# Hybrid decoder block with a mixture of experts: the final norm of all rows started before the last item's result, the last item's rows normed apart and scattered into the output

## What is computed

```python
x = x + mixed @ w_out[l]
x = x + moe(rms_norm(x, norm_ffn_g[l]), router_w[l], ...)   # top 4 of 32 experts
return rms_norm(x, final_norm_g)
...
gu = xb @ w_gu[e] + b_gu[e]
glu = jnp.minimum(gu[:, :D_FF], SWIGLU_LIMIT)
lin = jnp.clip(gu[:, D_FF:], -SWIGLU_LIMIT, SWIGLU_LIMIT)
act = glu * jax.nn.sigmoid(SWIGLU_ALPHA * glu) * (lin + 1)
return act @ w_down[e] + b_down[e]
```

## Time and profile before

| | us |
|---|---|
| median of 3 runs | 2394.51 (2391.37 to 2397.74) |
| the profiled execution, its own time | 2396.7 |
| its span | 2395.0 |
| TensorE matmul busy | 2314.8 (97%) |
| VectorE busy | 762.6 (32%) |
| ScalarE busy | 612.7 (26%) |
| GpSimd busy | 252.7 (11%) |
| clock that TensorE was granted, mean share | 0.987 |

### The profile page before, as it was taken

One profiled execution on the slowest core, in us unless ns is written; L12 is line 12 of the kernel. 1 busy time (PEld: TensorE's weight loads), 2 busy tenths in 40 slices (PEclk: granted clock), 3 DMA queues, 4 the chain that ended last, 5 costly groups with the idle time before them and its releaser, 6 DMA issues.

```text
span 2395.0 us, 41347 instructions
## 1 busy us (share of the span) xinstructions
PE 2314.8 (97%) x15446; PEld 1990.1 (83%) x15447; DVE 762.6 (32%) x1822; ACT 612.7 (26%) x1286; POOL 252.7 (11%) x231
## 2 busy tenths in 40 slices
PE   7999999999999999999999999999999999999993
PEld 4444554556589999999999999989999999999993
DVE  2342222678552233223322233212222222232222
ACT  2123121344312222222222232212222222222223
POOL 1000000111220010011001010000000000011001
PEclk9999999999999999999999999999999999999997
DMA  8000000211178999899898699846877787798785
GB/s 292 35 1 0 0 36 35 95 54 51 51 253 246 287 293 297 267 291 295 279 282 282 216 291 299 290 138 204 283 231 229 228 274 241 238 292 273 220 257 198
DMA packets 440781, 486.44 MB, mean 203 GB/s; under 512 B 24316, under 2 KB 417708, under 8 KB 440700
## 3 DMA queue, kind: packets, MB, share of 16 engines
q1 hardware_dynamic: 420140, 450.33, 57.2%
q0 software_dynamic: 20368, 35.29, 7.1%
q10 hardware_dynamic: 224, 0.16, 0.0%
HBM read 474.49 MB, written 49.58 MB: 219 GB/s over the span
## 4 chain that ended last, share of the span: by engine, by line
PE 95%; issue 2%; DVE 1%; DMA 1%; ACT 1%; POOL 0%; SPq 0%; ACTq 0%; POOLq 0%; DVEq 0%
PE PS L989 66%; PE PS L626 14%; PE PS L822 5%; PE PS L955 2%; PE PS L913 2%; PE PS L795 1%; PE PS L762 1%; PE PS L784 1%; PE PS L707 0%; PE PS L704 0%; PE PS L841 0%; DMA out_dram<-unit 0%; DVE unit L1489 0%; PE PS L662 0%; PE PS L599 0%
## 5 line engine op out<-in xcount | busy, mean ns | idle before, releaser
L989 PE MATMUL PS<-pairA,unit 128*128 x12288 | 1583.6, 291 | 13.8 <-issue 12.3
L989 PEld LDWEIGHTS PS<-pairA,unit 128*128 128x128 f32 x12288 | 1557.1, 191 | 34.3 <-issue 22.6
L626 PE MATMUL PS<-pairA,unit 128*128 128x512 f32 (+1 forms) x528 | 233.4, 598 | 2.8 <-issue 2.8
L1752 DVE TENSOR_SCALAR unit<-PS,cur_b 128x256 f32<-128x256 f32 x256 | 112.1, 480 | 353.3 <-PE PS L989 353.2
L1267 ACT ACTIVATE unit<-PS,cur_b 128x256 f32<-128x256 f32 x256 | 107.5, 471 | 454.9 <-PE PS L989 454.9
L542 POOL DMA_INDIRECT unit<-h_dram,cur_x x66 | 68.5, 1038 | 1301.6 <-DVE cur_x L1748 1212.9
L1254 ACT ACTIVATE unit<-unit 128x512 f32<-128x512 f32 x128 | 80.7, 631 | 466.0 <-DVE unit L1752 466.0
L626 PEld LDWEIGHTS PS<-pairA,unit 128*128 128x128 f32 (+1 forms) x528 | 97.9, 189 | 120.8 <-issue 120.1
L1258 ACT ACTIVATE unit<-PS,cur_b 128x256 f32<-128x256 f32 x256 | 107.5, 471 | 316.1 <-PE PS L989 316.1
L1759 DVE TENSOR_SCALAR unit<-unit 128x512 f32<-128x512 f32 x128 | 54.7, 427 | 339.5 <-ACT unit L1258 339.2
L1741 DVE COPY cur_b<-b_all 128x24 f32 x32 | 5.7, 178 | 437.7 <-ACT unit L1267 433.8
(11 more groups left out here) (242 smaller groups left out, 1257.5 us busy)
## 6 DMA issues: line engine op xcount, KB each, us to landing
unit<-in_expert_w_gu_dram SPq DMA_DIRECT2D x256, 1024.0 KB, 5.3
unit<-in_expert_w_down_dram SPq DMA_DIRECT2D x128, 1024.0 KB, 6.9
unit<-in_w_in_dram SPq DMA_DIRECT2D x6, 2048.0 KB, 15.4
pairB<-in_x_dram SPq DMA_DIRECT2D x16, 512.0 KB, 6.7
unit<-in_w_out_dram SPq DMA_DIRECT2D x2, 2048.0 KB, 9.5
h_dram<-pairA SPq DMA_DIRECT2D x8, 512.0 KB, 2.6
acc_dram<-pairB SPq DMA_DIRECT2D x8, 512.0 KB, 3.5
pairB<-acc_dram SPq DMA_DIRECT2D x8, 512.0 KB, 7.4
```

The source lines that it names most:

```text
L626: ins = pe.matmul(ps, lhs, rhs, start=(k == 0), stop=(k == KD - 1))
L989: ins = pe.matmul(bank(s)[:, ITEM * j:ITEM * j + w], slot_w[s][:, k, P * j:P * j + P], xa_cols[:, ITEM * k:ITEM * k + KD * ITEM + w][:, ba ...
L1752: ins = dve.tensor_scalar(glu_t[:, c % 2, ITEM * j:ITEM * j + ITEM], bank(gate_slot)[:, ITEM * j:ITEM * j + ITEM], cur_b[:, 2 * c + j:2 * ...
```

## The change

- SyncE waits for `y_sent` of last + 1 instead of last + 2 before the tail's loads: for all scatters but the one with the last item's result.
- That last scatter is gone. GpSimd instead gathers the last item's rows from `acc_dram` into SBUF (`last_rows`, cleared by a memset near the start of the items). VectorE adds the last result times the gate there straight from PSUM (`add_last`, four pieces of 512), after the norm of tile 4. ScalarE squares these rows, VectorE and GpSimd make their factors, VectorE scales them into `last_out`, and after all 8 tiles' stores have landed GpSimd scatters them into the output, over the rows that the tiles' stores wrote without the last item's share.
- VectorE itself squares and sums tiles 0 to 4 (`tensor_tensor_reduce`); ScalarE does tiles 5 to 7.
- In `one_pass` the registers and turns now stand in front of the pass's matmuls instead of behind them: no turn before pass 0, `turn_y` before pass 1, `turn_rows` before pass 2. The order of matmuls and turns on TensorE is thereby the same as before.
- The last `turn_y` is written out twice: directly behind the loop where there are no further items, and behind the code for them.

```diff
-            sp.wait_ge(y_sent, last + 2)
+            sp.wait_ge(y_sent, last + 1)
...
-            scatter(last)
+            pool.wait_ge(cur_y_ready, last + 1)
+            pool.sem_inc(pool_waited, 1)
+            for b in range(2):
+                pool.indirect_dma_start(
+                    out=last_rows[:, b, :], out_offset=None, in_=acc_dram,
+                    in_offset=bass.IndirectOffsetOnAxis(ap=cur_y[:, b:b + 1], axis=0),
+                    bounds_check=last_x, oob_is_err=False).then_inc(xg_in, 16)
             for t in range(NT):
                 pool.wait_ge(mean_sq, 3 * NT + t + 1)
...
+            pool.wait_ge(mean_sq, 4 * NT + 1)
+            pool.tensor_tensor(small[:, 4:6], small[:, 0:2], neg_half[:, 0:2], ALU.pow).then_inc(rstd_ready, 1)
+            for i in range(3):
+                pool.wait_ge(out_sent[i], 16 * len(range(i, NT, 3)))
+            for b in range(2):
+                pool.wait_ge(out_ready, NT + b + 1)
+                pool.sem_inc(pool_waited, 1)
+                pool.indirect_dma_start(
+                    out=out_flat, out_offset=bass.IndirectOffsetOnAxis(ap=cur_y[:, b:b + 1], axis=0),
+                    in_=last_out[:, b, :], in_offset=None,
+                    bounds_check=last_x, oob_is_err=False).then_inc(y_out, 16)
...
             def one_pass(widths):
+
+                p = pe.snap(phase, min_val=0, max_val=2)
+                with pe.If(p < 1):
...
+                with pe.Else():
+                    nxt = pe.snap(item, min_val=1, max_val=ITEMS)
+                    with pe.If(p < 2):
...
+                            turn_y()
...
+                    with pe.Else():
...
+                            turn_rows(nxt)
...
                 by_width(n, widths, four_slabs)
...
+            def turn_last():
+                pe.wait_ge(rhs_ready, 8 * last + 4)
+                for s in range(SLOTS):
+                    pe.wait_ge(bank_read[s], 48 * last + 16)
+                turn_y()
...
-            with pe.If(last > N_EXP):
+            with pe.If(last <= N_EXP):
+                turn_last()
+            with pe.Else():
...
+                turn_last()
...
-            take_y(last)
-
-            for t in range(NT):
+            for t in range(DVE_TILES, NT):
                 act.wait_ge(rows_in[t], 32)
...
+            for b in range(2):
+                act.wait_ge(last_summed, 2 * b + 2)
+                act.wait_ge(sum_squared, NT - DVE_TILES + b)
+                act.activation(sum_squares[:, 1, :], last_rows[:, b, :], ACT.Square,
+                               accum_out=small[:, b:b + 1]).then_inc(sum_squared, 1)
...
+            def add_last():
+
+                dve.wait_ge(xg_in, 32 * last + 96)
+                dve.wait_ge(g_ready, last + 1)
+                for q in range(4):
+                    dve.wait_ge(y_ps, 4 * last + q + 1)
+                    rows = last_rows[:, q // 2, HALF * (q % 2):HALF * (q % 2) + HALF]
+                    dve.scalar_tensor_tensor(out=rows, in0=bank(4 + q), scalar=g_now[:, q // 2, :], in1=rows,
+                                             op0=ALU.mult, op1=ALU.add).then_inc(last_summed, 1)
...
                 tail_norm(t)
+                if t == DVE_TILES - 1:
+                    add_last()
```

More of the change, by code:

```diff
@@ L89, in build @@
     out_rows = out.rearrange("b (t p) d -> (b t) p d", p=P)
+    out_flat = out.rearrange("b s d -> (b s) d")
     w_in_k = w_in.rearrange("l (k p) n -> p (l k) n", p=P)
@@ L551, in _ @@
             gather(0)
+            pool.wait_ge(xT_ps, 4)
+            step.do(pool.memset(last_rows, 0.0))
             pool.wait_ge(items_ready, 2)
@@ L970, in _ @@
                 "n_last", "n_now", "n_next", "phase", "moved", "first_six", "all_eight", "half", "pe_item"))
-            pe.load(n_now, item_n[0:1, 0:1])
-            pe.reg_mov(n_last, SEQ)
-            for reg, value in ((moved, 16), (first_six, 4), (all_eight, 4), (half, 0), (phase, 0), (item, 0), (n_next, 0)):
+            pe.load(n_next, item_n[0:1, 0:1])
+            pe.reg_mov(n_now, SEQ)
+            for reg, value in ((moved, 16), (first_six, 4), (all_eight, 0), (half, 0), (phase, 0), (item, 0), (n_last, SEQ)):
                 pe.reg_mov(reg, value)
             def one_pass(widths):
+                p = pe.snap(phase, min_val=0, max_val=2)
+                with pe.If(p < 1):
+                    pe.reg_mov(n_last, n_now)
+                    pe.reg_mov(n_now, n_next)
+                    pe.reg_add(item, item, 1)
+                    pe.reg_add(all_eight, all_eight, 4)
+                    pe.reg_mov(first_six, all_eight)
+                    pe.reg_mov(half, 0)
+                    pe.reg_mov(phase, 1)
+                with pe.Else():
+                    nxt = pe.snap(item, min_val=1, max_val=ITEMS)
+                    with pe.If(p < 2):
+                        n_done = pe.snap(n_last, min_val=0, max_val=SEQ)
+                        with pe.If(n_done <= P):
+                            turn_y(1)
+                        with pe.Else():
+                            turn_y()
+                        pe.load(n_next, item_n[0:1, bass.ds(nxt, 1)])
+                        pe.reg_mov(phase, 2)
+                    with pe.Else():
+                        n_after = pe.snap(n_next, min_val=0, max_val=SEQ)
+                        pe.wait_ge(y_evac, 4 * nxt)
+                        with pe.If(n_after <= P):
+                            turn_rows(nxt, 1)
+                        with pe.Else():
+                            turn_rows(nxt)
+                        pe.reg_add(first_six, all_eight, 3)
+                        pe.reg_add(all_eight, all_eight, 4)
+                        pe.reg_mov(half, KD * ITEM)
+                        pe.reg_mov(phase, 0)
                 n = pe.snap(n_now, min_val=0, max_val=SEQ)
@@ L1785, in tail_norm @@
                                          in1=gain_wide, op0=ALU.mult, op1=ALU.mult).then_inc(out_ready, 1)
+            def add_last():
[6 more added lines that the diff above has]
+                                             op0=ALU.mult, op1=ALU.add).then_inc(last_summed, 1)
+            step.base, step.n = start + per_item * last, 0
             tail_mean(0)
@@ L1791, in _ @@
                 tail_norm(t)
+                if t == DVE_TILES - 1:
+                    add_last()
+            dve.wait_ge(sum_squared, NT - DVE_TILES + 2)
+            dve.tensor_scalar(small[:, 0:2], small[:, 0:2], 1.0 / D, EPS, ALU.mult, ALU.add).then_inc(mean_sq, 1)
+            dve.wait_ge(rstd_ready, 4 * NT + 1)
+            for b in range(2):
+                dve.scalar_tensor_tensor(out=last_out[:, b, :], in0=last_rows[:, b, :], scalar=small[:, 4 + b:5 + b],
+                                         in1=gain_wide, op0=ALU.mult, op1=ALU.mult).then_inc(out_ready, 1)
 _INS = ['x', 'norm_attn_g', 'w_in', 'rel_bias_table', 'lambda_q1', 'lambda_k1', 'lambda_q2', 'lambda_k2',
```

55 lines of the change are left out of this document (15 added, 40 removed).

## The result

| | before | changed |
|---|---|---|
| median (range), runs side by side, us | 2395.59 (2391.37 to 2397.74) | 2370.93 (2369.10 to 2374.75) |
| the profiled execution, its own time | 2396.7 | 2369.1 |
| its span | 2395.0 | 2367.3 |
| first matmul of the first pass | 673.3 | 674.6 |
| end of the last pass's matmuls | 2354.3 | 2337.9 |

The ratio is 0.9898 [0.9885, 0.9910]: 24.7 us faster between the medians, where 11.0 were forecast. The last two lines split the difference of the spans, 27.7 us: 11.3 lie in the tail, 16.4 ahead of it. The forecast had all of its 11.0 in the tail and nothing ahead.

The account below looks back on a forecast made before the run. TensorE, busy 97% of the span, was taken as the bound, leaving gains in the 40.7 us tail: -20.7 (loads) + 2.7 (additions) + 7.0 (end) = -11.0 us, from 2394.5 to 2383.5; range 2377.5 to 2391.0.

Parts of the forecast that it names:

- Turns in front: 0 on the chain: TensorE's item loop: same turns, matmuls and branches per pass, so 0 us, as far as the branches find their code.
- A: TensorE's item loop: one or two more stalls, 2388.6 to 2393.7, chance 0.13; one or two fewer, 2373.3 to 2378.4, chance 0.08.
- sign of being wrong: TensorE within the items: the prediction is wrong if the number of "issue" stretches over 3 us isn't four.
- Against: ... the first visit to a wide body ..., which the new layout has too: Evidence against more stalls: three of four mark a wide body's first visit or first way out, which the new layout keeps.
- Loads 20.7 us earlier, SyncE's loop late next: Tail: loads move from 2368.4 to 2347.7, 20.7 us earlier, then held by SyncE's loop for items that aren't there.
- VectorE's squares at 1.3 us: Tail: VectorE squares and sums tiles 0 to 4 at 1.3 us each, costing nothing; next bound if loads came faster.
- The additions at 2.7: Tail: four PSUM pieces at 0.68 us on VectorE between the norms of tiles 4 and 5, adding 2.7 us.
- The end: After the last store: 0.75 us to the first scatter, 1.87 to the second, 4.39 to landing, 7.0 us new; then 0.4.
- The exit at 0: TensorE's last turn behind the exit branch: up to 4.4 us sooner, but worth 0 because VectorE reaches the addition later.
- Rival C: TensorE's item loop: a usual pass's code no longer stays at hand; one stall per item is 163 us, 2547; chance 0.05.

Follow-up runs that it names:

- the skip: The changed kernel with SyncE going over its loop for absent items by one branch instead of through it 15 times: 2363.63 us, ratio to before 0.9862.
- the skip and 67 instructions: The changed kernel with SyncE's empty loop skipped and 67 never executed instructions ahead of TensorE's item loop: 2363.69 us, ratio to before 0.9866.
- 195 instructions: The changed kernel with SyncE's empty loop skipped and 195 never executed instructions ahead of TensorE's item loop: 2369.98 us, ratio to before 0.9890.

## Why the prediction was wrong

Its tail was right in sum, to 0.3 us (11.3 against 11.0); the time fell below the range because of one step.

- **"Turns in front: 0 on the chain" failed.** The turns in front give 17.7 us in the items, less 1.4 us by which the first pass starts later, behind its new stall. The runs with the turns in front alone and with turns and exit (2381 and 2379) show it, and the new tail alone (2385.1, the forecast's 11.0) shows that nothing else is missing. The prediction had the right sentence beside it ("as far as the branches find their code") and the right rival: A, its better side, "One or two fewer". Its sign of being wrong came as well: four stretches over 3 us were forecast within the items, and there are two (4.96 and 4.38), with one of 2.96. Two of the stalls did vanish, and were worth 12.7 us where 10.2 stood, since the second one's cost had been read only against its slower neighbour: both passes of width 256 were slow, 30.56 and 29.57 against 27.8. A's case of two fewer was 2373.3, with 0.08 for the side.
- **What no term or rival held** were the small pieces of the items, 7.7 us together, 4.4 of them at pass 0 of 19 items. A view would have told of a part: of the "issue 12.3" in the group of L989, two stalls of the earlier trace rows are 8.5 us, and the other 3.8 stand in nine small waits, of which 1.1 in five are left now.
- **"Against: ... the first visit to a wide body ..., which the new layout has too"** was wrong as evidence. The new layout visits the body of 256 rows for the first time as well, and has no stall there; the kernel before has none there either with 131 dead instructions ahead of its loop.
- **Loads 20.7 us earlier, SyncE's loop late next: right.** Cutting the loop short is worth 5.9 us in the tail, which shows that it was the bound.
- **VectorE's squares at 1.3 us: right**, 1.23 + 0.08 us. **The additions at 2.7: right**, 2.72 on the path. The forecast had VectorE's squares as the next bound if the loads came faster. The skip bears that out: there VectorE is busy nearly throughout, and the norm of tile 3 waits for GpSimd.
- **The end: right in sum, by luck.** The first scatter started 0.8 us after the last store had landed (2356.6 + 2.7), near the 0.75 us forecast, though the row of L606 names VectorE's norm as its releaser. The last scatter started 1.35 us after the first instead of 1.87, and landed 2.2 us after its start, where 4.39 stood. What fills the time from there to the end of the span is no transfer but GpSimd's closing DRAIN, of which no term spoke; 0.4 us stood for all that comes after the landing. In the kernel before it took longer, but ran beside the last stores (rows below). From the last scatter's start to the end of the span it took 5.8 us, where 4.4 + 0.4 stood: two errors that nearly cancel.
- **The exit at 0: right** in the new tail. **Rival C** didn't happen, but exists: 260 instructions more in the loop and it is there.
- **The range**: its lower end, 2377.5, lay below either case that is named for it (2378.4 and 2379.1); the measured time lies 6.6 us below that end.

GpSimd's closing DRAIN (ns, and its start), first in the changed kernel, then in before:

```profile
L102 POOLq DRAIN  x1: 3253/3253/3253, 2363.8 to 2363.8; - x1
```

```profile
L101 POOLq DRAIN  x1: 4437/4437/4437, 2389.2 to 2389.2; - x1
```

## What to carry to other kernels

Where an engine runs a long loop with branches, its code is a resource with a price: look for idle stretches whose only reason is "issue", count them and their small kin by group, and expect an edit that reorders code to move them, in either direction and by more than the edit's own purpose. Test it with instructions that never run. When a wait is taken away, ask what the waiting engine does before it reaches that point: here an empty loop of 7 us, free until then, became the first term of the tail. And when an engine's last instruction moves to the very end, look at what that engine still does behind it.

## What was not expected of the hardware

- A stall costs more than its gap: the two at width 256, 8.5 us of idle, were worth 12.7 together with the slower passes behind them, in which the granted clock was 0.51 and 0.83 at first.
- TensorE goes 96 times through a loop of some 1,475 instructions with 7 fetches within the items, and with 260 more in the loop 226 further blocks are fetched and 584 us lost.
- GpSimd's closing DRAIN behind its last scatter took 3.25 us at the very end of the span.
- A part of the spread lies far ahead of the change. In the profiled execution with the skip, 2368.6 us, the granted clock was low once more at 154 us, and its first pass started 4.9 us later than with the skip and 67 instructions (2364.06). The windows from 150 to 165 us, first the former, then the latter:

```profile
150.00:165.00 15.00, 15.00 (x42) 6.33 (x40) 1.23 (x1) 2.82 (x4) 0.00 (x0) 0.77 0.00 0
```

```profile
150.00:165.00 15.00, 15.00 (x48) 6.52 (x47) 1.23 (x1) 5.65 (x8) 0.00 (x0) 1.00 0.00 0
```

The other three runs with the skip took 2363.3 to 2363.7. The profiled execution with 195 instructions had 0.77 in this window as well, which fits the rest of its later first pass. What sets that moment off wasn't tried.
